# Who makes the second pair's two raw low parts at the switch to block products: GpSimd or VectorE

## The reference, cut to what matters

```
def swiglu(x, w_gu, w_down):
    gate, up = jnp.split(x @ w_gu, 2, axis=-1)
    return (jax.nn.silu(gate) * up) @ w_down

x = x + 0.5 * rmsnorm(swiglu(rmsnorm(x, n[0]), w1_gu[l], w1_down[l]), n[1])
m, S_a, S_r = mixer(rmsnorm(x, n[2]), ...)
x = x + rmsnorm(m, n[3])
x = x + 0.5 * rmsnorm(swiglu(rmsnorm(x, n[4]), w2_gu[l], w2_down[l]), n[5])
```

## Time and profile before

| | us |
|---|---|
| median of 3 runs | 2154.8 (2154.28 to 2155.37) |
| profiled execution, whole | 2155.37 |
| profiled execution, span of the profile | 2153.6 |
| TensorE busy | 2114.0 (98%) |
| VectorE busy | 1309.5 (61%) |
| ScalarE busy | 941.5 (44%) |
| GpSimd busy | 862.3 (40%) |

### The profile page before, as it was taken

One profiled execution on the slowest core, in us unless ns is written; L12 is line 12 of the kernel. 1 busy time (PEld: TensorE's weight loads), 2 busy tenths in 40 slices (PEclk: granted clock), 3 DMA queues, 4 the chain that ended last, 5 costly groups with the idle time before them and its releaser, 6 DMA issues.

```text
span 2153.6 us, 43008 instructions
## 1 busy us (share of the span) xinstructions
PE 2114.0 (98%) x17095; PEld 2086.0 (97%) x17095; DVE 1309.5 (61%) x1995; ACT 941.5 (44%) x1727; POOL 862.3 (40%) x708
## 2 busy tenths in 40 slices
PE   8999999999999999999999999999999999999998
PEld 8999999999989999999999999999999899999998
DVE  5988700587368888840189885007863788888202
ACT  5455433442344554543354444234424454544333
POOL 3433344443315433344544334453432345233442
PEclk9999999999999999999999999999999999999999
DMA  5234442322234233442423345332222343344422
GB/s 151 79 106 131 142 144 85 94 79 74 65 97 137 70 89 115 132 157 86 117 61 89 109 124 169 115 110 65 81 68 60 97 138 89 89 119 122 156 87 75
DMA packets 389341, 224.54 MB, mean 104 GB/s; under 512 B 9780, under 2 KB 380264, under 8 KB 387880
## 3 DMA queue, kind: packets, MB, share of 16 engines
q1 hardware_dynamic: 372208, 213.19, 33.5%
q10 hardware_dynamic: 16952, 8.81, 1.4%
HBM read 200.41 MB, written 21.56 MB: 103 GB/s over the span
## 4 chain that ended last, share of the span: by engine, by line
PE 89%; DVE 6%; issue 2%; ACT 1%; POOL 1%; DMA 0%; SPq 0%; DVEq 0%; POOLq 0%; ACTq 0%
PE ps L715 54%; PE ps L772 29%; PE ps L947 1%; DVE x L1992 1%; DVE y L1986 1%; DVE xb L1797 1%; POOL w_lo L636 1%; DVE xs_lo L1748 1%; PE ps L1109 0%; PE ps L1126 0%; PE ps L1021 0%; ACT o_hi L1627 0%; DMA x_tok<-in_x_prompt_dram 0%; DVE ps L1838 0%; PE ps L1048 0%
## 5 line engine op out<-in xcount | busy, mean ns | idle before, releaser
L636 POOL TENSOR_TENSOR w_lo<-raw,w_hi 128x384 fp32r<-128x384 f32 (+1 forms) x452 | 558.8, 1246 | 676.0 <-ACT w_hi L1315 675.9
L1315 ACT ACTIVATE w_hi<-raw 128x384 fp32r<-128x384 f32 (+1 forms) x452 | 246.8, 559 | 455.6 <-PE ps L715 451.8
L772 PE MATMUL ps<-xb,w_hi 128*128 128x272 f32 x2048 | 393.6, 290 | 7.5 <-DVE w_lo L1852 7.4
L715 PE MATMUL ps<-xs_hi,w_hi 128*128 128x288 f32 (+1 forms) x1568 | 345.0, 292 | 4.7 <-DVE xs_lo L1748 4.2
L715 PE MATMUL ps<-xs_hi,w_lo 128*128 128x288 f32 (+1 forms) x1568 | 340.6, 288 | 0.0
L715 PE MATMUL ps<-xs_lo,w_hi 128*128 128x288 f32 (+1 forms) x1568 | 339.7, 288 | 0.0
L772 PEld LDWEIGHTS ps<-xb,w_hi 128*128 128x128 f32 x2048 | 326.4, 191 | 9.1 <-DVE w_lo L1852 8.2
L772 PE MATMUL ps<-xb,w_lo 128*128 128x272 f32 x1024 | 298.2, 291 | 0.0
L715 PEld LDWEIGHTS ps<-xs_hi,w_hi 128*128 128x128 f32 x1568 | 257.2, 189 | 12.0 <-DVE xs_lo L1748 6.2
L715 PE MATMUL ps<-h_hi,w_lo 128*128 128x256 f32 x1272 | 267.2, 289 | 0.0
L715 PE MATMUL ps<-h_lo,w_hi 128*128 128x256 f32 x1272 | 266.1, 288 | 0.0
(11 more groups left out here) (264 smaller groups left out, 3768.2 us busy)
## 6 DMA issues: line engine op xcount, KB each, us to landing
raw<-in_w_gu_dram SPq DMA_DIRECT2D x176, 512.0 KB, 4.1
raw<-in_w_in_dram SPq DMA_DIRECT2D x56, 512.0 KB, 3.7
raw<-in_w_down_dram SPq DMA_DIRECT2D x64, 384.0 KB, 3.4
raw<-in_w_down_dram SPq DMA_DIRECT2D x64, 320.0 KB, 3.2
h_away<-low_away SPq DMA_DIRECT2D x44, 272.0 KB, 4.4
h_lo<-h_away SPq DMA_DIRECT2D x8, 1088.0 KB, 7.7
raw<-in_w_out_dram SPq DMA_DIRECT2D x16, 512.0 KB, 3.9
ret_state<-in_state_ret_dram SPq DMA_DIRECT2D x8, 512.0 KB, 6.5
```

Source lines behind the costliest of these rows:

```text
L636: pool.tensor_tensor(lo, raw[:, u, k0:k0 + n, :], hi.bitcast(F32), ALU.subtract)\
L715: mm = pe.matmul(bank_part(bank, a), w, v[:, k, TOK[a]], start=(start and n == 0), stop=(stop and n == 2))
L772: mm = pe.matmul(ps[:, j, 0:TH], w[j][:, k, :], xb[:, c_, part, k, :], start=(k == 0 and m == 0), stop=(k == KH - 1 and m == 2))
L1315: act.activation(hi, raw[:, u, k0:k0 + n, :], ACT.Copy).then_inc(hi_split, 1)
```

## The change

The low parts (1, 0) and (1, 1) of each half go from GpSimd's list to VectorE's. VectorE makes them behind the four sums and c12, ahead of the low parts of terms 2 to 5. GpSimd's wait for the last `xb_low` goes with them. The two signals' counts follow. Two lines fall away, so line numbers from 683 on are lower by 2 in the changed kernel.

```diff
--- before.py
+++ after.py
@@ -335,7 +335,7 @@
         xb_high, xb_ready = sig("xb_high", 2 * NTERM), sig("xb_ready", 2 * NTERM)
         pair_loaded = [sem(f"pair_loaded{u}") for u in range(UNITS)]
         sum_ready, term_high, term_done = sig("sum_ready", 2 * NPAIR * 4), sig("term_high", 2 * NPAIR * NTERM), sig("term_done", 2 * NPAIR * NTERM)
-        outer_ready, inner_ready = sig("outer_ready", 2 * (3 * NPAIR - 1)), sig("inner_ready", 2 * (4 * NPAIR + 1))
+        outer_ready, inner_ready = sig("outer_ready", 2 * (3 * NPAIR - 3)), sig("inner_ready", 2 * (4 * NPAIR + 3))
         kept_ready, c_ready = sig("kept_ready", 2 * NPAIR), sig("c_ready", 2 * NPAIR * len(C_ORDER))
         pair_silu, h_made = sig("pair_silu", 2 * NPAIR), sig("h_made", 2 * NPAIR)
         sent_away, fetched = sem("sent_away"), [sem(f"fetched{i}") for i in range(3)]
@@ -407,8 +407,8 @@
             eng.wait_ge(pair_loaded[u], 16 * ((2 * l + f) * (NPAIR // 2) + n // 2 + 1))
 
         HIGH_ORDER = ((4, 6, 0, 1, 5, 2, 3), (0, 1, 2, 3, 4, 5, 6))
-        DVE_LOWS = ((0, 4), (0, 6), (0, 5), (0, 2), (0, 3)) + tuple((n, j) for n in range(1, NPAIR) for j in (2, 3, 4, 5))
-        POOL_LOWS = ((0, 0), (0, 1), (1, 0), (1, 1)) + tuple(
+        DVE_LOWS = ((0, 4), (0, 6), (0, 5), (0, 2), (0, 3), (1, 0), (1, 1)) + tuple((n, j) for n in range(1, NPAIR) for j in (2, 3, 4, 5))
+        POOL_LOWS = ((0, 0), (0, 1)) + tuple(
             (m, j) for n in range(1, NPAIR) for m, j in ((n, 6), (n + 1, 0), (n + 1, 1)) if m < NPAIR)
         SUM_ORDER = (3, 1, 2, 4)
         SUM_TERM = {1: 3, 2: 2, 3: 4, 4: 5}
@@ -680,8 +680,6 @@
                             wait_sum(pool, l, f, n + 1, 1)
                         elif j == 6:
                             wait(pool, h_ready, l, f * KF + TILE0 + n - 1)
-                        elif (n, j) == (1, 0):
-                            wait(pool, xb_ready, l, f * NTERM + NTERM - 1)
                         term_low(l, f, n, j)
                     with pool.Fori(0, DOWN_GROUPS - 1) as i:
                         group(l * GROUPS + DOWN[f] + i, DOWN_KT)
@@ -1936,7 +1934,7 @@
                     for i in SUM_ORDER:
                         term_sum(l, f, 1, i)
                     take_c(l, f, n, "c12")
-                    for j in (2, 3, 4, 5):
+                    for j in range(6):
                         term_low(l, f, 1, j)
 
             def up(l, f):
```

## The result

The changed kernel takes 2158.9 us (median of 15 runs, 2156.3 to 2162.0), the kernel before 2155.1 (15 runs, 2154.3 to 2155.9). The ratio is 1.0018, 95% interval 1.0011 to 1.0025: 3.8 us slower, between 2.4 and 5.4. The forecast was +5.4 (2160.2), and the result lies in the range of 2156.5 to 2164.3. The prediction did not foresee the spread: 6 us instead of 1.6.

A forecast was written before the change was run, and what follows sets the result against it. TensorE's own work plus its stops was taken to bound the kernel. Later starts of term 2 at four switches, +5.4 us, clock and later work at nothing, gave 2160.2 us from the median 2154.8; range 2156.5 to 2164.3.

The forecast's parts named there:

- Step 1: VectorE at a switch: first to third sum takes 1.43 us without GpSimd, instead of 2.66, a gain of 1.23.
- Rival (d): GpSimd is not what slows VectorE's first two sums; each moved low part comes 1.23 us later: 2165.1, chance 0.03.
- Step 2: A moved low part takes 0.70 us on VectorE, so TensorE stands 3.2 us ahead of term 0.
- Steps 3 and 4: Term 2 of the second pair starts 1.40 us later at the first switch; all four switches sum to +5.4.
- Step 5: TensorE's clock falls at every switch, costing 1.66 us each already; the change was taken to add nothing.
- rival (a): Clock falls at switches partly in idle time or missing: 2158.6 with none missing, 2155.2 with two, chance 0.35.
- rival (b): The clock stays low longer at one or more switches: 2161.9 to 2167.0 us, chance 0.16.
- Step 6: Behind the switch: no later VectorE work is delayed, and TensorE's 1.4 us delay stays 1.4 us.
- Rival (c): Faster: term 0 ready when TensorE arrives, so stops and clock falls go, 14.0 us, 2140.8; chance 0.03.

The follow-up runs named there:

- e6: The kernel before with 4 float32 matmuls of 240 columns, results unread, in TensorE's stop of 1.8 us: 2155.1 us, ratio 0.9998.
- e5: The changed kernel with 7 float32 matmuls of 256 columns, results unread, in TensorE's stop of 3.16 us: 2153.7 us, ratio 0.9991.
- e8: The kernel before, both low parts on GpSimd, with the four sums of pair 1 in the order 1, 2, 4, 3: 2150.5 us, ratio 0.9977.
- e1_half: Half of the change to the kernel before: (1, 0) stays on GpSimd, (1, 1) goes to VectorE behind c12: 2153.1 us, ratio 0.999.
- e2_first: The changed kernel with the two moved low parts ahead of VectorE's four sums: 2155.6 us, ratio 1.0000.
- e9_changed_again: The changed kernel measured again without an edit: 2159.1 us, ratio 1.0016 to the kernel before.

## Why the prediction was right, and where its steps were off

- **Step 1**, sums without GpSimd: 1.43 us from first to third sum forecast, 1.42 measured (102.75 to 104.17); first sum to moved low part 3.23 forecast, 3.21 measured. Rival (d) is out.
- **Step 2**, the moved low part: bounds 0.65 and 0.83, taken 0.70; the two take 1.28 together, 0.68 for one. TensorE's stop was forecast at 3.2 us and is 3.15 to 3.16.
- **Steps 3 and 4**: no stop ahead of term 2. At the second switch, where the clock stays up, it is 7.06 us from the first sum to term 2 (783.07 to 790.13), 6.99 forecast, 5.60 before: a delay of 1.46. Terms 0 and 1 take 3.10 us there, not 3.01.
```profile
783.07 0.69 DVE L1841 TENSOR_TENSOR ps<-raw 128x512 f32<-128x512 f32 x1
...
787.03 0.52 PE L770 MATMUL ps<-xb,w_hi 128*128 128x272 f32 x2 [3.15 <-DVE w_lo L1850]
...
790.13 0.42 PE L770 MATMUL ps<-xb,w_hi 128*128 128x272 f32 x2
```
- **Step 5, the clock, was mis-sized in two ways,** and came out near nothing in the sum by luck. The falls of the kernel before were priced at 1.66 each, because term 2 to pair 2 took that much longer than at full clock. That is true and yet they cost the kernel nothing: e6 without them has stretches of the same length. And in the changed kernel falls are not as regular as I took them: in its two profiled executions they came at two and at three of the four switches, once of double length. So rival (a), with missing falls, and rival (b), with a longer low stretch, both occur in executions of one program. Without falls the changed kernel is 1.9 us faster (e5), with three, one of them double, 3.0 us slower in the profiled span (2156.6 against 2153.6). No profile shows the falls of the median execution of 2158.9; four low stretches of 3.4 us at the switches are what its mean clock of 0.995 fits, an estimate.
- **Step 6 failed in its mechanism**: "In the pairs behind, TensorE is never last to be served, so 1.4 us of delay on TensorE stays as 1.4 us." Before, VectorE was later than TensorE at pair 2. Pair 2 took 10.81 us where it takes 10.55 in the changed kernel (118.77 to 129.31), so 0.26 us of stop went away with TensorE's delay. And the fall costs less after the change: it begins 0.25 us before TensorE does (from the share 0.72 at about 106.45, and 106.70), and terms 0 and 1 take 4.52 us with it (106.70 to 111.22) against 3.10 without, 1.42 where it was 1.66 before. From term 2's delay of 1.46, less 0.26, less 0.24, comes 0.96; the first switch measured 0.98. Four times 1.0 is 4.0 if all four fall once, and the measured median is +3.8. The list of waits could not show what lay under the falls: a stop that a fall covers is in no row. The 0.26 the trace did show, as a wait of the weight load in pair 2, which the list cut to PE leaves out (first the kernel before, then the changed one at term 2 of pair 1 and at pair 3):
```profile
120.27 0.30 PEld L772 LDWEIGHTS ps<-xb,w_hi 128*128 128x128 f32 x2 [0.21 <-DVE late_lo L1852]
```
```profile
111.22 0.42 PE L770 MATMUL ps<-xb,w_hi 128*128 128x272 f32 x2
...
129.31 0.41 PE L770 MATMUL ps<-xb,w_hi 128*128 128x272 f32 x2
```

  Where the clock stays up, still more goes. From term 2 of pair 1 to pair 3 it is 19.99 us in e6 (107.94 to 127.93) and 18.09 in the changed kernel (111.22 to 129.31). So 1.90 us of waiting on VectorE and GpSimd lay behind term 2, more than the whole delay of 1.46; in the kernel before, the falls covered 1.6 of it.
- **The sign hangs on the falls.** I had VectorE some 0.3 us earlier behind the switch, and that as worth nothing (step 6, "no later work of VectorE is delayed"). It is 0.45 us earlier, and where the clock stays up the stretch is 0.43 us shorter (173.08 in e6, 172.65 in e5), which is why e5 is 1.9 us faster than the kernel before. The prediction had the loss come from the later term 2 alone, whatever the clock does. Rival (c) asked whether the low part is done by 103.1, and was right that it isn't; it overlooked that VectorE's end, not TensorE's start, could set the pairs.

So the sign came out and the number lies in the range, with 1.4 a switch in the sum where the runs show some 1.0 for a switch with one fall and a gain of some 0.4 for one without. Steps 1 to 4 were right by their mechanism. (The terms of the range's upper end add up to 9.3, not 9.5, which changes nothing here.) That a loss was left at all is the work of falls of the clock with TensorE last behind them, which the prediction had at nothing, and in that part it was lucky.

## What to carry to other kernels

A wait that the profile names is only the first of those that bind; take it away on paper and look at what engine arrives next, and when. Here two engines reached the second pair within a few tenths of a microsecond of each other, so neither a shorter stop nor a clock that stays up was worth its face value, while 1.43 us off VectorE's queue (e8, 7.90 to 6.47) made the stretch 1.41 us shorter. An edit that lets a full queue run ahead of a long stop also trades a steady time for one that depends on the clock: look at the spread and at each run's mean clock, not at the median alone.

Before work is moved off an engine that holds another up, try another order: of the two instructions that collided with GpSimd's (both with two operands in SBUF), one had room behind them, and the other lost its wait by starting just ahead of GpSimd's, which at one switch of four it did not.

## What the runs showed of the hardware

- A fall of the clock does not follow from a stop's length alone. Stops of 3.15 and 3.16 us in one execution gave a fall twice and none twice; stops of 1.8 us before gave one each time in the profiled execution and, by the clocks of single runs (up to 1.000), none in others. A stop of 1.80 us at the fourth switch of e1_half gave none, nor did the four of 1.55 to 1.57 in e2_first. A stop of 2.44 us in the mixer was passed over before; in the changed kernel the clock fell within the same stop, there 2.45 us.
- The low stretch at a switch was 3.4 us long in every profiled case but one, where it was 6.8 (104.98 to 111.82 in e9_changed_again, from the shares of the windows), behind a stop of the same 3.16 us.
- VectorE's subtraction of two SBUF operands into SBUF takes 0.68 us for 128x512, the same as with one operand in PSUM. Beside GpSimd's subtraction of two SBUF operands it is a matter of who starts first: the sum that began at 103.08 in the earlier trace rows ended 0.6 us behind GpSimd's end, while in e8_order_before the sum got through at 102.54 in 0.70 us and GpSimd's two low parts took 3.08 us together, where two undisturbed ones of the changed kernel took 2.55. The Trainium skill ("SBUF — State Buffer", Who interferes with whom) calls what the two engines share an exclusive lock, and says that the order of issue decides which of them blocks; both cases agree.
- A float32 matmul of 256 columns from plain float32 operands took 0.44 us of TensorE (28 in 12.25), against 0.125 for one of 272 columns on float32r, both at 2.4 GHz.
